# First norm's root multiplied to the outputs of the first projection, with the skewed bias loaded by SyncE's queue and one pooling sum moved later

## The reference, cut to what matters

```python
def rms_norm(x, g):
    xf = x.astype(jnp.float32)
    y = xf * lax.rsqrt(jnp.mean(xf * xf, axis=-1, keepdims=True) + EPS)
    return (y * g.astype(jnp.float32)).astype(x.dtype)
...
        h = rms_norm(x, norm1_g[l])
        y = h @ w_in[l]                    # 1024 -> 1280
        q = y[..., :D_ATTN]                # 512, 8 heads of 64
        k = y[..., D_ATTN:D_ATTN + D_KV]   # 128
        v = y[..., D_ATTN + D_KV:D_ATTN + 2 * D_KV]
        p = y[..., D_ATTN + 2 * D_KV:]     # 512, 4 pooling groups
        a = swa_attention(q, k, v, q_norm_g[l], k_norm_g[l], attn_sinks[l], rel_bias)
        b = pool_mixer(p, pool_w[l], pool_scale[l])
        x = x + jnp.concatenate([a, b], axis=-1) @ w_out[l]
```

## Time and profile before

| | |
|---|---|
| median of 3 runs | 3212.59 us |
| the runs | 3221.16, 3212.59, 3207.81 us |
| the profiled execution's own time | 3216.56 us |
| its span, first to last instruction | 3214.8 us |
| mean granted TensorE clock | 0.975 |
| TensorE busy in the span | 3026.0 us (94%) |

### The profile page before, as it was taken

How to read it: one execution, slowest core, us unless ns; L and a number is a source line. 1 busy time by engine, 2 the same in 40 slices (tenths; PEclk the granted TensorE clock), 3 DMA queues, 4 the chain that set the end, 5 groups by cost and what they waited for, 6 DMA issues and landing times.

```text
span 3214.8 us, 43511 instructions
## 1 busy us (share of the span) xinstructions
PE 3026.0 (94%) x15596; PEld 2532.2 (79%) x15596; DVE 1808.2 (56%) x3028; ACT 1111.1 (35%) x1568; POOL 1431.9 (45%) x1692
## 2 busy tenths in 40 slices
PE   6799999999999999999998988776999998999999
PEld 4697668888888889999997786333988886898887
DVE  5758884555555526778887625787433334343333
ACT  4432233444444433333334423454322223231221
POOL 4344344444444446877741223000455554645553
PEclk9899999999999999999999999887999999999999
DMA  5123785555555568999995211000232222232222
GB/s 166 40 86 107 280 282 190 184 184 183 184 183 184 183 210 296 329 335 362 352 362 208 67 47 66 1 0 27 86 98 98 94 95 79 92 98 89 103 92 79
DMA packets 214456, 498.48 MB, mean 155 GB/s; under 512 B 83224, under 2 KB 101784, under 8 KB 211736
## 3 DMA queue, kind: packets, MB, share of 16 engines
q1 hardware_dynamic: 86688, 310.64, 28.6%
q10 hardware_dynamic: 105080, 118.50, 10.7%
q0 software_dynamic: 22528, 67.19, 5.8%
HBM read 431.78 MB, written 64.49 MB: 154 GB/s over the span
## 4 chain that ended last, share of the span: by engine, by line
PE 77%; DVE 10%; DMA 4%; ACT 3%; POOL 2%; issue 2%; another core or an unknown queue 1%; SPq 0%; ACTq 0%; DVEq 0%
PE ps L572 23%; PE ps L574 23%; PE ps L573 23%; PE ps L785 3%; PE ps L753 1%; POOL picked L532 1%; DVE nb L1869 1%; POOL value_rows L540 1%; DMA abuf<-act_dram 1%; DMA rel_dram<-relv 1%; DVE stats L1888 1%; DMA unit_raw<-w_units 1%; DVE Ed L1914 1%; PE ps L965 1%; ACT Ed L1413 1%
## 5 line engine op out<-in xcount | busy, mean ns | idle before, releaser
L514 POOL TENSOR_TENSOR unit_lo<-unit_raw,unit_hi 128x256 fp32r<-128x256 f32 x1432 | 1065.3, 779 | 1595.7 <-ACT unit_hi L1057 1595.0
L572 PE MATMUL ps<-hn_hi,unit_hi 128*128 128x512 f32 (+1 forms) x2344 | 921.4, 393 | 26.3 <-DVE hn_lo L1526 15.4
L573 PE MATMUL ps<-hn_lo,unit_hi 128*128 128x512 f32 (+1 forms) x2344 | 897.0, 383 | 0.0
L574 PE MATMUL ps<-hn_hi,unit_lo 128*128 128x512 f32 (+1 forms) x2344 | 896.5, 382 | 0.0
L1057 ACT ACTIVATE unit_hi<-unit_raw 128x1024 fp32r<-128x1024 f32 x486 | 505.8, 1055 | 424.1 <-DMA unit_raw<-w_units 293.7
L572 PEld LDWEIGHTS ps<-hn_hi,unit_hi 128*128 128x128 f32 x2344 | 443.5, 189 | 156.3 <-issue 46.1
L574 PEld LDWEIGHTS ps<-hn_hi,unit_lo 128*128 128x128 f32 x2344 | 443.3, 189 | 86.1
L573 PEld LDWEIGHTS ps<-hn_lo,unit_hi 128*128 128x128 f32 x2344 | 444.2, 189 | 82.4 <-issue 3.8
L572 PE MATMUL ps<-gp_hi,unit_hi 128*128 128x384 f32 x1024 | 346.2, 338 | 15.7 <-DVE gp_lo L1802 11.5
L574 PE MATMUL ps<-gp_hi,unit_lo 128*128 128x384 f32 x1024 | 344.3, 336 | 0.9 <-issue 0.9
L573 PE MATMUL ps<-gp_lo,unit_hi 128*128 128x384 f32 x1024 | 344.4, 336 | 0.7 <-issue 0.7
(11 more groups left out here) (261 smaller groups left out, 4280.0 us busy)
## 6 DMA issues: line engine op xcount, KB each, us to landing
unit_raw<-w_units SPq DMA_DIRECT2D x486, 512.0 KB
araw<-ada_units SPq DMA_DIRECT2D x96, 512.0 KB, 6.0
act_dram<-stage ACTq DMA_DIRECT2D x32, 1024.0 KB, 6.6
gate_dram<-gst ACTq DMA_DIRECT2D x16, 1536.0 KB, 6.4
gbuf<-gate_dram ACTq DMA_DIRECT2D x32, 768.0 KB
abuf<-act_dram ACTq DMA_DIRECT2D x32, 768.0 KB
x<-x_t SPq DMA_DIRECT2D x8, 256.0 KB, 6.1
picked<-act_dram,act_at POOLq DMA_INDIRECT x128
```

What stands on the lines that cost most here:

```text
L514: last = nc.gpsimd.tensor_tensor(lo[:, u % RING, cols], raw[:, u % RING, cols], hi[:, u % RING, cols].bitcast(F32), ALU.subtract)
L572: mm(dst, wh, ah, start=start, stop=False)
L573: mm(dst, wh, al, start=False, stop=False)
L574: return mm(dst, wl, ah, start=False, stop=stop)
```

## The change

The product with `rstd` leaves the inputs of the projection and goes to its outputs, since each token's root is one factor of all its outputs.

- Inputs: `hn_hi` is now `x * gain` (ScalarE, `row_high`), `hn_lo` its low part (VectorE), with no root in them. The squares are taken after that, and the chain of squares, sum, average and root runs beside the first two units.
- TensorE takes the averages after unit 1 (`token_means`): the product with `ones` as before, and four matmuls of one column that give the same averages with tokens on the partitions, for v. The small matmul of the bias follows there. The five sums by head are taken one unit later (n = 2 to 6 in place of 1 to 5).
- Outputs: VectorE takes the banks of n = 0 to 8, times `rstd` (`evict`). ScalarE squares what was taken, roots it (`head_root`), and takes bank 9 in four pieces with the root of its tokens as scale. For each n ScalarE's `split_hi` now comes before its other work.
- SyncE's queue: parameters and unit 0 first, then constants, x, units 1 to 7. It also loads the skewed bias, after unit 14, waiting for the store there.
- The pooling sum of group 3 moves from before `band_max(0)` to after `band_share(1)`, ahead of `band_low(0)`.

```diff
+            sp.dma_start(par[:, :], params).then_inc(params_in, 16)
+            load_unit(0)
             sp.dma_start(con[:, :], consts).then_inc(consts_in, 16)
             for c in range(DC):
                 sp.dma_start(x[:, c], x_in[:, c]).then_inc(x_loaded[c], 16)
-            sp.dma_start(par[:, :], params).then_inc(params_in, 16)
-            for u in range(RING):
+            for u in range(1, RING):
                 load_unit(u)
...
-            load_range(RING, U_PEER + RING)
+            load_range(RING, U_WIN + 15)
+            sp.wait_ge(rel_stored, 16)
+            sp.dma_start(bias[:, :, :], ...).then_inc(bias_in, 16)
+            load_range(U_WIN + 15, U_PEER + RING)
...
+            def token_means():
+                pe.wait_ge(consts_in, 16)
+                pe.wait_ge(sq_added, DC - 1)
+                mm(ps[:, 7, :], ones, std[:, :], start=True, stop=True)
+                for t in range(TT):
+                    last = mm(ps[:, 5, t:t + 1], std[:, t * P:(t + 1) * P], ones[:, 0:1], start=True, stop=True)
+                last.then_inc(mean_ready, 1)
...
-                if 1 <= n <= 5:
-                    pe.wait_ge(win_sq, n)
-                    mm(ps[:, 4 + (n - 1) % 2, :], blocks, sq[:, (n - 1) % 2, :], start=True, stop=True)\
-                        .then_inc(win_bs, 1)
+                if n == 1:
+                    token_means()
+                    relative_bias()
+                if 2 <= n <= 6:
+                    pe.wait_ge(win_sq, n - 1)
+                    mm(ps[:, 4 + n % 2, :], blocks, sq[:, n % 2, :], start=True, stop=True).then_inc(win_bs, 1)
...
+            split_hi(0)
             act.wait_ge(consts_in, 16)
-            norm(0, squares=True, ahead=range(AHEAD))
+            activation(rstd[:, 0:1], eps, ACT.Sqrt)
+            act.wait_ge(params_in, 16)
+            for c in range(DC):
+                row_high(c)
+                if c == 4:
+                    split_hi(1)
+            for c in range(DC):
+                square(0, c)
+                if c == 3:
+                    split_hi(2)
+            split_hi(3)
+            act.wait_ge(mean_ready, 1)
+            activation(std[:, :], ps[:, 7, :], ACT.Sqrt, bias=eps, scale=P / D)
+            activation(rcol[:, 0:TT], ps[:, 5, 0:TT], ACT.Sqrt, bias=eps, scale=P / D).then_inc(std_ready, 1)
+            split_hi(4)
...
             for n in range(10):
                 used(U_WIN + n)
+                split_hi(U_WIN + n + AHEAD)
                 if n < 5:
+                    act.wait_ge(win_ev, n + 1)
                     if n >= 2:
+                        head_root(n - 2)
+                    activation(sq[:, n % 2], qT[:, n] if n < 4 else kT[:, :], ACT.Square).then_inc(win_sq, 1)
+                if n in (5, 6):
+                    head_root(n - 2)
+                if n == 9:
+                    act.wait_ge(rstd_ready, 1)
+                    for t in range(TT):
+                        last = activation(vS[:, t, :], ps[:, n % 4, t * P:(t + 1) * P], ACT.Copy,
+                                          scale=rcol[:, TT + t:TT + t + 1])
+                    last.then_inc(win_v, 1)
...
+            for c in range(DC):
+                dve.wait_ge(hn_hi_ready, c + 1)
+                V.scalar_tensor_tensor(hn_lo[:, c], x[:, c], pc("norm1", c, 1), hn_hi[:, c].bitcast(F32), ALU.mult,
+                                       ALU.subtract).then_inc(hn_ready, 1)
+            for c in range(1, DC):
+                square_sum(0, c)
...
+            for n in range(9):
+                evict(n)
+                if 2 <= n <= 6:
+                    head_scale(n - 2)
+                if n == 8:
+                    dve.wait_ge(bias_in, 16)
+                    dve.wait_ge(con2_in, 32)
+                    link(V.tensor_tensor(bias[:, :, :], ...))
+                if n >= 6:
+                    pool_sums(n - 6)
...
             band_max(0)
-            dve.wait_ge(unit_used, U_WIN + 10)
             band_max(1)
             band_share(0)
             for t in range(2):
                 band_max(t + 2)
                 band_share(t + 1)
+                if t == 0:
+                    pool_sums(3)
+                    dve.wait_ge(pool_d, 4)
                 band_low(t)
```

More of the change, by code:

```diff
@@ L171, in build_program @@
         kT = at("swa_k", R2 + 8 * KB, [P, T])
+        rcol = at("token_rstd", R2 + 28 * KB, [P, 8])
         vS = at("swa_v", R2 + 10 * KB, [P, TT, P])
@@ L319, in build_program @@
         rel_mm = sem("rel_mm")
+        win_v, rstd_ready = sem("win_v"), sem("rstd_ready")
         win_ev = sem("win_ev")
@@ L466, in _ @@
             sp.dma_start(poolw[:, :, :], pool_w).then_inc(con2_in, 16)
-            load_range(RING, U_PEER + RING)
+            load_range(RING, U_WIN + 15)
+            sp.wait_ge(rel_stored, 16)
+            sp.dma_start(bias[:, :, :], rel_dram[:, P - 1:P - 1 + P * (REL - 1)].rearrange(
+                "h (q r) -> q h r", r=REL - 1)[:, :, 0:BAND]).then_inc(bias_in, 16)
+            load_range(U_WIN + 15, U_PEER + RING)
             def load_ada(m, i=None):
@@ L644, in seam_units, with relative_bias @@
                             seam_mean(k, 1)
[L646 to L652, removed]
+            def token_means():
[5 more added lines that the diff above has]
+                last.then_inc(mean_ready, 1)
+            def relative_bias():
+                pe.wait_ge(params_in, 16)
+                pe.wait_ge(con2_in, 32)
+                mm(ps[0:HEADS, 6, 0:REL], pc("rel_bias")[0:32, :], con2[0:32, 0:REL], start=True, stop=True)\
+                    .then_inc(rel_mm, 1)
             def band_scores(t):
@@ L660, in band_scores @@
                 elif t == 1:
-                    pe.wait_ge(win_ev, 10)
+                    pe.wait_ge(win_ev, 9)
+                    pe.wait_ge(win_v, 1)
                 else:
@@ L1065, in square @@
                 if k == 0:
-                    act.wait_ge(x_loaded[c], 16)
+                    act.wait_ge(hn_hi_ready, c + 1)
                 elif k != 3:
@@ L1084, in norm @@
                 for c in range(DC):
-                    act.wait_ge(nrm_ready, DC * WHOLE[k] + c + 1)
+                    act.wait_ge(nrm_ready, DC * (WHOLE[k] - 1) + c + 1)
                     if shift is None:
@@ L1144, in seam, with row_high, head_root @@
                     seam_high(k, 1, c)
-            act.wait_ge(consts_in, 16)
-            norm(0, squares=True, ahead=range(AHEAD))
+            def row_high(c):
+                act.wait_ge(x_loaded[c], 16)
+                activation(hn_hi[:, c], x[:, c], ACT.Identity, scale=pc("norm1", c, 1)).then_inc(hn_hi_ready, 1)
+            def head_root(m):
+                act.wait_ge(win_bs, m + 1)
+                if m >= 2:
+                    act.wait_ge(qn_done, m - 1)
+                activation(nrm[:, m % 2], ps[:, 4 + m % 2, :], ACT.Sqrt, bias=eps, scale=P / HD).then_inc(win_std, 1)
+            split_hi(0)
+            act.wait_ge(consts_in, 16)
+            activation(rstd[:, 0:1], eps, ACT.Sqrt)
[13 more added lines that the diff above has]
+            split_hi(4)
             act.wait_ge(rel_mm, 1)
@@ L1156, in _ @@
                 used(U_WIN + n)
-                bank = ps[:, n % 4, :]
+                split_hi(U_WIN + n + AHEAD)
                 if n < 5:
+                    act.wait_ge(win_ev, n + 1)
                     if n >= 2:
[L1160 to L1177, removed]
+                        head_root(n - 2)
[8 more added lines that the diff above has]
+                    last.then_inc(win_v, 1)
             def pool_high(g):
@@ L1610, in _, with evict, head_scale, pool_sums @@
             dve.wait_ge(params_in, 16)
[L1611 to L1617, removed]
-                                       ALU.mult).then_inc(qn_done, 1)
[L1621 to L1627, removed]
+            for c in range(DC):
[4 more added lines that the diff above has]
+                square_sum(0, c)
+            V.memset(E[0][:, :, 0:P], LOW)
+            dve.wait_ge(std_ready, 1)
+            link(V.reciprocal(rstd[:, :], std[:, :]))
+            V.reciprocal(rcol[:, TT:2 * TT], rcol[:, 0:TT]).then_inc(rstd_ready, 1)
+            def evict(n):
+                dve.wait_ge(unit_used, U_WIN + n + 1)
+                dst = qT[:, n] if n < 4 else kT[:, :] if n == 4 else pT[:, n - 5]
+                V.tensor_tensor(dst, ps[:, n % 4, :], rstd[:, :], ALU.mult).then_inc(win_ev, 1)
+            def head_scale(m):
+                dve.wait_ge(win_std, m + 1)
+                link(V.reciprocal(nrm[:, m % 2], nrm[:, m % 2]))
+                dst = qT[:, m] if m < 4 else kT[:, :]
+                dve.wait_ge(win_ev, m + 1)
+                V.scalar_tensor_tensor(dst, dst, pc("qg" if m < 4 else "kg"), nrm[:, m % 2], ALU.mult,
+                                       ALU.mult).then_inc(qn_done, 1)
+            def pool_sums(g):
+                w = POOL_WINDOWS[g]
                 dve.wait_ge(win_ev, 6 + g)
@@ L1639, in _ @@
```

(7 more changed lines are left out.)

## The result

| | before | after |
|---|---|---|
| median | 3221.26 us (20 runs, 3204.9 to 3237.23) | 3203.34 us (20 runs, 3192.52 to 3219.59) |
| ratio of the runs | | 0.9948, 95% interval 0.9933 to 0.9964 |
| profiled execution: time, span | 3216.56, 3214.8 us | 3211.59, 3209.8 us |
| first matmul of the output projection | 155.21 us | 137.56 us |

By the ratio the change is worth 0.52% (0.36 to 0.67), some 16.8 us; forecast were 18.75 us, 0.58%. The forecast time of 3193.8 and its range of 3184 to 3203 were missed all the same, by 0.34 us at the range's end: the median of before was 3212.59 over three runs, on which the forecast stood, and is 3221.26 over twenty. In two later sets of runs of the same kernel it was 3215.59 (13 runs) and 3211.77 (23 runs), so even the median of twenty moves by up to 9.5 us from set to set.

What follows compares the result with a forecast made beforehand. Bounds: TensorE waiting for chunks, then busy to unit 9, then a four-engine chain in the band. band_max(1) 20.5 us earlier less 1.75 for the moved sum gives 18.75; 3212.59 - 18.75 = 3193.8 us, range 3184 to 3203.

Steps and rivals of the forecast that it cites:

- The anchor: Time forecast taken from the before kernel's median of 3212.59 us, said to have some 3 us of its own.
- The start: Unit 0 on TensorE: starts at 11.0 in place of 26.9 us, last chunk's matmuls end near 20.5.
- The prediction's estimate from that price: ScalarE's two table loads at the skill page's price: 2.8 us more, chunk 5 later by 1.2 to 1.5 us.
- The averages: TensorE after unit 1: last sum at 26.8, averages at 29.4, unit 2 starts at 30.1 us.
- the columns: TensorE's four one-column averages for v, two weight loads each: 0.41 us a pair, 1.64 in all.
- The bounds for unit 2: Unit 2's start on TensorE: 28.4 us below (27 with unit 0's gaps halved), 35.5 and a little over above.
- The turn into the band: From unit 9's end at 85.1: split_hi(14) 1.06, v 0.9, scores 2.0, so band_max(1) at 89.0, 20.5 us earlier.
- The moved sum: Group 3's pooling sum ahead of band_low(0): tile 1's transposes 1.75 us later; bounds 1.75 and 4.06.
- The bias: Skewed bias: store issued at 31.8, load at 65.4, landed 72.4; VectorE asks at 75.5, 3.1 us of slack.
- rival with a late bias: Bias landing beyond 77.5 us costs its full delay; chance 0.08 late but not slower, 0.02 slower than before.
- Half a per cent: Whole kernel: faster by over 0.5%, a gain over 16.1 us, at chance 0.66; within 0.5% 0.32, slower 0.02.

Runs made afterwards that it cites:

- a1: The changed kernel with the skewed bias's load back on ScalarE between n = 3 and n = 4; output projection at 148.6 us.
- a3: The changed kernel with ScalarE's pieces of v ahead of split_hi of unit 14; output projection at 136.5 us.
- a4: The changed kernel with split_hi of unit 1 behind the eighth row_high, not the fifth; output projection at 137.9 us.
- run 13: Not a run's label: the text says that a unit "can run 13 of its 24 matmuls at the lower clock".
- a6_pool_mid: The changed kernel with group 3's pooling sum between band_max(0) and band_max(1); output projection at 135.15 us.

## Why the prediction was right or wrong

**The anchor, the step that failed.** The prediction put its gain under "the median of the runs" and allowed it "some 3 us of its own". That median moved by 8.7 us, to 3221.26, as three runs became twenty, and it was 3215.59 and 3211.77 in the later sets. The five profiles show where such a spread can come from: the stage of the values alone ran from 595.9 to 609.8 us in unchanged code. The prediction's own sum, 18.75 us, taken from 3221.26 gives 3202.5, 0.8 us from the measurement. The range was built from the bounds of the edit's costs and gave 3 us to the median, where it needed 8 to 9; why the medians of whole sets differ is open.

**The start: right, early by 1 us.** First matmul forecast 11.0, measured 9.96: the first table load ran at 0.75, before anything had landed, and not behind unit 0. Chunk 5 is held up by unit 1's load as said (13.99, forecast 14.5), unit 1 starts at 19.59 (20.5), the last sum is there at 26.4 (26.8). Both table loads took 1.28 us and the activation behind the second came at 7.73, directly at its end (6.43 + 1.28), so the price of 2.66 us for a switch in the Trainium skill ("ScalarE: Activation LUTs", What ACT_TABLE_LOAD costs) is not seen here. The prediction's estimate from that price, chunk 5 later by 1.2 to 1.5 us, does not follow from its own terms either: 9.9 + 2.8 for the first input and four more at 0.63 is 15.2, against unit 1 at 14.5, which makes it 0.7, again as an estimate.

**The averages: the columns overpriced.** Four one-column products took 0.79 us in the chain, not 1.64. Unit 2 starts at 29.1, not 30.1, and unit 9 ends at 83.9, not 85.1; the 55.0 us between are 54.8. The bounds for unit 2 were added up loosely: the lower comes to 28.7 by its own terms, not 28.4, and the upper to 37.2 with averages at twice their 2.5 us, not 35.5. VectorE kept up, with 0.97 us of waiting for each root. It was through `band_max(0)` at 83.8, 3 us before the forecast.

**The turn into the band: order right, clock not.** `split_hi(14)` 1.06 and v 1.04 stand in the chain as forecast (1.06 and 0.9). The scores were priced at 2.00, the price of the higher clock; they took 3.79, 2.00 and 2.48. `band_max(1)` at 89.98, 88.21 and 89.12, forecast 89.0.

**The moved sum: mis-sized.** "1.75 us later, and all behind with them". Like with like it is 6.4 us. The wait of the transposes was foreseen, but its length was read against scores that ended at 127.69 in the first profile of before, 18.2 us behind its `band_max(1)`, the latest of all fourteen profiles. Tile 0's transposes and the scores had run at the lower clock there (2.84 and 3.79 us). In the three profiles of the changed kernel the scores end 16.0 to 16.3 us behind `band_max(1)`, so TensorE waits 3.8 to 4.0 us (and 2.2 to 2.5 in a1, a3 and a4, where they end at 17.6 to 17.9). What the wait does to the clock of the next two groups, 3.4 us, was not in the sum. It did not show in the total because the same first profile had its own band at a granted clock of 0.74: 45.7 us from `band_max(1)`, where kernels with the sum early take 42.7 in the mean. That the two errors met, 47.4 forecast and 47.6 to 48.6 measured, is luck.

**The bias: right.** Store issued at 30.60 (31.8), load at 64.23 (65.4), so 33.6 us once more, and landed 5.7 us later, at 69.9 (72.4). VectorE's mask follows its eviction at 72.6 (75.5) without a wait. The slack was 2.7 us (3.1), and no rival with a late bias came up.

**Half a per cent.** 0.66 stood on faster by over 0.5%. The ratio 0.9948 is there by 0.02%, with an interval over both sides.

## What to carry to other kernels

An instruction that is moved "into the shade" has to be checked against who waits for the instructions behind it: ahead of `band_low(0)` the sum cost 6.4 us, behind it 1 to 3, and in VectorE's own gap (6.2, 4.4 and 4.9 us in three executions) next to nothing. In a stage where TensorE comes and goes, a gap is priced with what it can do to the next matmuls' clock, and the kernel before should be read in two or three profiles, since its one profile may be the slow draw of that stage. A forecast in microseconds is only as good as the median that it stands on; give the ratio from the traces, and put the spread of the medians into the range.

## What the runs showed of the hardware that was not expected

- Products of one column (fp32, 128 by 128 weights): eight records in 0.79 to 0.95 us, some 0.1 us each.
- The granted clock in the band varies between executions of one kernel: 0.80, 0.82 and 0.80 behind `band_max(1)` in the three profiles of the changed kernel, 0.74 and 0.81 in two of the kernel before. The same 16 scores behind the same gap of 2.3 us took 2.0 to 3.8 us.
- A unit behind the one-column products can run 13 of its 24 matmuls at the lower clock (a6_pool_mid), though TensorE had no gap over 1.3 us before. It was so in one of eleven profiles.
- The first matmuls of a program can be at the lower clock where the window's granted clock reads 1.00: in the window from 9.90 to 19.60 the first nine, to 13.51, stand 0.42 to 0.56 us apart, and those from 13.78 to 14.94 only 0.22 to 0.24. At the start the spacing tells the level, the column does not.
- The broadcast store of 1536 KB from 8 partitions took 33.6 us in both kernels, though it started at 39.98 us in one and at 30.60 in the other.
